# Head products that take both halves of x in one pass, in halves of 256 columns

## What is computed

```python
z = rms_norm(x, norm_mix) @ w_in      # first block, 2048 -> 5144 columns
# columns: gMLP 1024, dilated attention 3 x 512, NSA queries 1024,
#          keys and values for compression 512, selection 512, window 512, gates 24
# later: cross attention (q from x, k and v from mem), MLP of 8192
p_lat = h_lat @ w_in_2                # second block: HGRN2 queries 1024, gates, values, ...
```

## Time and profile before

| | |
|---|---|
| median of 3 executions | 2600.96 us (2600.3 to 2600.99) |
| the profiled execution | 2600.4 us, span 2598.6 us |
| TensorE busy | 2576.3 us, 99% |
| VectorE, ScalarE busy | 1838.8 us (71%), 1361.8 us (52%) |
| moved by DMA | 582.98 MB, mean 224 GB/s |

### The profile page before, as it was taken

The page is one execution under the profiler, slowest core; times in us unless marked ns, Lnnn a source line. Parts: engine busy times, 40 slices in busy tenths (PEclk is TensorE's granted clock), DMA queues, the critical chain, the costliest instruction groups (busy, mean ns, idle before and its releaser), DMA issues.

```text
span 2598.6 us, 35433 instructions
## 1 busy us (share of the span) xinstructions
PE 2576.3 (99%) x13200; PEld 2173.1 (84%) x13200; DVE 1838.8 (71%) x3327; ACT 1361.8 (52%) x2613; POOL 176.9 (7%) x233
## 2 busy tenths in 40 slices
PE   8999999999999999999999999999999999999999
PEld 7999889888888888888888898888788888888887
DVE  5677665777799999676867775677866665555555
ACT  5445575655545445455766566565544444444443
POOL 1011100021100000000011100000001111000000
PEclk9999999999999999999999999999999999999999
DMA  9796665688888888866777755544577777565564
GB/s 304 236 296 184 209 202 171 188 287 278 290 284 270 277 285 271 308 191 219 237 242 236 247 175 153 156 131 153 162 233 257 255 253 224 186 195 188 188 193 161
DMA packets 315707, 582.98 MB, mean 224 GB/s; under 512 B 30176, under 2 KB 38384, under 8 KB 315408
## 3 DMA queue, kind: packets, MB, share of 16 engines
q1 hardware_dynamic: 296768, 559.94, 66.0%
q0 software_dynamic: 18480, 20.47, 3.6%
q10 hardware_dynamic: 288, 0.31, 0.0%
HBM read 574.35 MB, written 2.10 MB: 222 GB/s over the span
## 4 chain that ended last, share of the span: by engine, by line
PE 96%; DVE 1%; ACT 1%; SPq 0%; DMA 0%; issue 0%; DVEq 0%; ACTq 0%
PE ps L1838 27%; PE ps L1840 26%; PE ps L1839 26%; PE ps L1827 3%; PE ps L1828 3%; PE ps L1829 3%; PE ps L1784 2%; PE ps L1920 1%; PE ps L1890 1%; PE ps L1909 1%; DMA raw<-in_w_in 0%; DVE wlo L2495 0%; PE ps L2035 0%; ACT whi L2157 0%; PE ps L2052 0%
## 5 line engine op out<-in xcount | busy, mean ns | idle before, releaser
L2495 DVE TENSOR_TENSOR wlo<-raw,whi 128x512 fp32r<-128x512 f32 x1712 | 1098.2, 686 | 536.5 <-ACT whi L2157 534.0
L2157 ACT ACTIVATE whi<-raw 128x512 fp32r<-128x512 f32 x1712 | 982.0, 624 | 817.1 <-PE ps L1840 527.1
L1838 PE MATMUL ps<-whi,th 128*128 128x512 f32 (+1 forms) x3124 | 1230.9, 394 | 2.2 <-ACT hA L2351 1.0
L1840 PE MATMUL ps<-whi,tl 128*128 128x512 f32 (+1 forms) x3124 | 1211.2, 388 | 0.0
L1839 PE MATMUL ps<-wlo,th 128*128 128x512 f32 (+1 forms) x3124 | 1210.3, 387 | 0.0
L1838 PEld LDWEIGHTS ps<-whi,th 128*128 128x128 f32 x3124 | 586.9, 188 | 122.2 <-issue 5.1
L1840 PEld LDWEIGHTS ps<-whi,tl 128*128 128x128 f32 x3124 | 586.5, 188 | 121.7
L1839 PEld LDWEIGHTS ps<-wlo,th 128*128 128x128 f32 x3124 | 587.4, 188 | 115.7 <-issue 1.0
L2513 DVE SCALAR_TENSOR_TENSOR acc<-raw,silc,acc 128x512 f32<-128x512 f32 x480 | 343.9, 746 | 10.5 <-DMA raw<-in_w_mod 6.0
L1827 PE MATMUL ps<-th,whi 128*128 128x256 f32 x640 | 186.0, 291 | 11.0 <-DVE wlo L2495 8.1
L1828 PE MATMUL ps<-th,wlo 128*128 128x256 f32 x640 | 181.6, 284 | 0.0
(11 more groups left out here) (320 smaller groups left out, 1296.7 us busy)
## 6 DMA issues: line engine op xcount, KB each, us to landing
raw<-in_w_in SPq DMA_DIRECT2D x231, 512.0 KB, 3.9
raw<-in_w_down SPq DMA_DIRECT2D x216, 512.0 KB, 4.6
raw<-in_w_mod SPq DMA_DIRECT2D x192, 512.0 KB, 4.5
raw<-in_w_gate_up SPq DMA_DIRECT2D x176, 512.0 KB, 3.5
raw<-in_w_up SPq DMA_DIRECT2D x128, 512.0 KB, 4.6
raw<-in_w_out SPq DMA_DIRECT2D x64, 512.0 KB, 3.8
raw<-in_xattn_wkv SPq DMA_DIRECT2D x16, 512.0 KB, 3.4
raw<-in_w_in SPq DMA_DIRECT2D x16, 268.0 KB, 4.1
```

Source lines behind the costliest of these rows:

```text
L1838: pe.matmul(p, xh, wh[:, c, c0:n], start=a and (form != "both" or tb == 0), stop=False, skip_group_check=True)
L1840: ins = pe.matmul(p, xl, wh[:, c, c0:n], start=False, stop=z, skip_group_check=True)
L2157: self.e.activation(t.his[g % NHI][:, n * c:n * c + n], t.raws[j % NRAW][:, n * c:n * c + n], ACT.Copy).then_inc(*s.hi.up((g, c)))
L2495: self.e.tensor_tensor(t.los[j % NRAW][:, at], t.raws[j % NRAW][:, at], t.his[g % NHI][:, at].bitcast(F), ALU.subtract).then_inc(*s.lo.up( ...
```

## The change

In form "heads" a gemm now walks its 512 columns in two halves of 256: each half runs over all 16 k-tiles with a pair of banks of its own, one head in each bank. `th` and `tl` lie in one tile (`thl`), so that one product with the standing `whi` moves 512 columns, th and tl of a k-tile: hi by hi lands in the first half of the bank, hi by lo (of x) in the second. A second product, of 256 columns, with `wlo` standing, adds to the first half. At the end of each half ScalarE copies the second half of each bank into the destination, VectorE adds the first, and then VectorE multiplies by the scales (or ScalarE applies silu). Chunks of 256 columns hold four k-tiles (the first two chunks: two), in rows of 1 KB. For cc the multiply by the scales is moved into `first_steps`, behind the spreading of the scales. "rows", "both" and "three" stay.

```diff
@@ gemm
+        if form == "heads":
+            for b in range(n // 256):
+                pair = self.take_pair()
+                epi(b, pair, self.part(op, w, row0, col0 + 256 * b, 256, kts, pair, form))
+            return
@@ part
-            m = 1 if self.small else min({512: 2, 536: 1}.get(n, len(kts)), len(kts) - i)
+            m = {512: 2, 536: 1, 256: 4}[n]
+            m = min(m // 2 if self.small else m, len(kts) - i)
@@ direct
-        def epi(pair, end):
-            for b in range(nh // 2):
-                self.heads_direct(name, b, pair, end, dst[:, h0 + 2 * b:h0 + 2 * b + 2, :], by, used)
-            pair.give((self.s.hx, (name, nh // 2 - 1)))
-            self.flags.add(name)
+        def epi(b, pair, end):
+            out = dst[:, h0 + 2 * b:h0 + 2 * b + 2, :]
+            self.heads_joined(name, b, pair, end, out, used)
+            pair.give((self.s.hj, (name, b)))
+            if late:
+                self.flags.add(f"{name} joined {b}")
+                return
+            self.heads_scaled(name, b, out, by)
+            if 2 * b + 2 == nh:
+                self.flags.add(name)
@@ first_steps
-            self.spread("x", op1.rs)
+            while not self.side_ready():
+                yield
+            bank = self.side().take()
+            self.spread_rstd("x", op1.rs, bank)
+            bank.give((s.sd, "x"))
+            yield from self.until("cc joined 1")
+            for b in range(2):
+                self.heads_scaled("cc", b, t.cc[:, 2 * b:2 * b + 2, :], op1)
+            self.flags.add("cc")
@@ Tensor.multiply
+        if form == "heads":
+            for c, kt in enumerate(kts):
+                self.wait_ge(*s.lo.at((g, c // 2)))
+                self.wait_all(op.ready[kt])
+                a, z = first and c == 0, last and c == len(kts) - 1
+                for h in range(2):
+                    hs = slice(128 * h, 128 * h + 128)
+                    pe.matmul(pair.tile[h][:, :], wh[:, c, hs], op.hl[:, :, kt, :], start=a, stop=False, skip_group_check=True)
+                    ins = pe.matmul(pair.tile[h][:, 0:S], wl[:, c, hs], op.h[:, kt, :], start=False, stop=z, skip_group_check=True)
+            ins.then_inc(*s.mm.up(j))
+            return
@@ Scalar
+    def heads_joined(self, name, b, pair, end, dst, used):
+        self.wait_all([end])
+        self.wait_all(used)
+        for h in range(2):
+            ins = self.e.activation(dst[:, h, :], pair.tile[h][:, S:2 * S], ACT.Copy)
+        ins.then_inc(*self.s.hb.up((name, b)))
+    def heads_silu(self, name, b, dst):
+        self.wait_ge(*self.s.hj.at((name, b)))
+        self.e.activation(dst, dst, ACT.Silu).then_inc(*self.s.hqs.up((name, b)))
@@ Vector
+    def heads_joined(self, name, b, pair, end, dst, used):
+        t, s = self.t, self.s
+        self.wait_ge(*s.hb.at((name, b)))
+        for h in range(2):
+            ins = self.e.tensor_tensor(dst[:, h, :], pair.tile[h][:, 0:S], dst[:, h, :], ALU.add)
+        ins.then_inc(*s.hj.up((name, b)))
```

More of the change, by code:

```diff
@@ L112, in __init__ @@
             new("turn_hi"), new("turn_lo"))
-        self.hqs = new("queries_silu")
+        self.hqs, self.hb, self.hj = new("queries_silu"), new("heads_second_half"), new("heads_joined")
         self.ro, self.hx = new("rows_copied"), new("heads_direct")
@@ L163, in __init__ @@
         self.name = name
-        self.h, self.l = tiles
+        self.h, self.l, self.hl = tiles
         self.ready = [[] for _ in range(16)]
@@ L239, in __init__ @@
         for n, at in (("1", r_1), ("2", r_2), ("3", z)):
[L240 removed]
+            both = sb("thl" + n, at, [2, 16, S], R)
+            self.op[n] = (both[:, 0, :, :], both[:, 1, :, :], both)
         self.yr = sb("yr", r_1 + 16384, [16, S])
@@ L770, in rows, with direct, epi @@
         return epi
-    def direct(self, name, dst, h0, by, nh=4, used=()):
-        def epi(pair, end):
-            for b in range(nh // 2):
-                self.heads_direct(name, b, pair, end, dst[:, h0 + 2 * b:h0 + 2 * b + 2, :], by, used)
-            pair.give((self.s.hx, (name, nh // 2 - 1)))
-            self.flags.add(name)
+    def direct(self, name, dst, h0, by, nh=4, used=(), late=False):
+        def epi(b, pair, end):
[8 more added lines that the diff above has]
+                self.flags.add(name)
         return epi
     def silu_heads(self, name, dst, used):
[L783 to L786, removed]
+        def epi(b, pair, end):
+            self.heads_joined(name, b, pair, end, dst[:, 2 * b:2 * b + 2, :], used)
+            self.heads_silu(name, b, dst[:, 2 * b:2 * b + 2, :])
+            pair.give((self.s.hj, (name, b)))
+            if b:
+                self.flags.add(name)
         return epi
@@ L1328, in run @@
         w_in = a["w_in"][0]
-        self.gemm(op1, w_in, 0, 3584, 512, range(16), self.direct("cc", t.cc, 0, op1), "heads")
+        self.gemm(op1, w_in, 0, 3584, 512, range(16), self.direct("cc", t.cc, 0, op1, late=True), "heads")
         self.spawn("big", self.compress())
@@ L1805, in multiply @@
         wh, wl = view(t.his[g % NHI], (len(kts), n)) if self.plan else None, view(t.los[j % NRAW], (len(kts), n)) if self.plan else None
-        heads = {"rows": 0, "heads": n // 128, "both": n // 256, "three": 2}[form]
+        heads = {"rows": 0, "heads": 2, "both": n // 256, "three": 2}[form]
         c0 = 128 * heads
@@ L2155, in split @@
             self.wait_ge(*signal.at(key))
-        for c in range(k):
-            self.e.activation(t.his[g % NHI][:, n * c:n * c + n], t.raws[j % NRAW][:, n * c:n * c + n], ACT.Copy).then_inc(*s.hi.up((g, c)))
+        u = 2 if n == 256 else 1
+        for c in range(0, k, u):
+            at = slice(n * c, n * (c + u))
+            self.e.activation(t.his[g % NHI][:, at], t.raws[j % NRAW][:, at], ACT.Copy).then_inc(*s.hi.up((g, c // u)))
     def stat(self, name, tb, src, landed, at):
@@ L2491, in split @@
         k, n = self.plan[j][2]
-        for c in range(k):
-            at = slice(n * c, n * c + n)
-            self.wait_ge(*s.hi.at((g, c)))
+        u = 2 if n == 256 else 1
+        for c in range(0, k, u):
+            at = slice(n * c, n * (c + u))
+            self.wait_ge(*s.hi.at((g, c // u)))
             self.e.tensor_tensor(t.los[j % NRAW][:, at], t.raws[j % NRAW][:, at], t.his[g % NHI][:, at].bitcast(F),
-                                 ALU.subtract).then_inc(*s.lo.up((g, c)))
+                                 ALU.subtract).then_inc(*s.lo.up((g, c // u)))
     def mod_add(self, jj, j, kc, vs):
```

11 lines of the change are left out of this document (6 added, 5 removed).

## The result

The changed kernel takes 2607.47 us (median of 9 runs, 2604.77 to 2608.98), the kernel before 2600.96 beside it (9 runs, 2600.2 to 2603.01). The ratio is 1.0025, with a 95% interval of 1.0016 to 1.0033: slower by 6.5 us, where no change was forecast, and 2.5 us above the upper end of the forecast range (2594.5 to 2605.0). The profiled execution took 2607.2 us (span 2605.4).

What follows compares the result with a forecast made beforehand. TensorE's products and waits were taken to bound the kernel. From 2600.4 us, +6.5 first gemm, -1.8 given back, +1.6 half rate, -6.8 other gemms make -0.5: 2599.9, stated as 2600.0 us; range 2594.5 to 2605.0.

Steps and rivals of the forecast that it cites:

- first gemm, with half rate: Start: last x part late, first product of rows 6.5 us later; 3.15 us at half rate after the idle, 1.6 us.
- wait for cb given back: At 46.63 us: TensorE's wait for blocks VectorE makes from cc goes, 1.8 us less (0 if VectorE is late).
- pairs of the eight other gemms: Gemms after the first: a pair takes 0.347 us where three products took 0.360; 512 x 0.0133 = 6.8 us less.
- query halves: Ends of the query gemms' halves: copies, additions and silu nearly hidden; 0 to 2 us a half, costed at nothing.
- 41.5 to 44: Sign for the forecast at the start: first product of rows comes at 41.5 to 44 us.
- rival A: First gemm: no late start, the whole product gain stays, 2592.7 us; chance 0.10.
- signs that were to show the prediction wrong: Pair step not 0.347, k-tiles 14 and 15 starting before 28, or new waits over 1 us behind query halves.
- rival B: Four query halves: ScalarE's queue of copies, table loads and silu outlasts the cover; 2 us each give 2608; chance 0.07.
- The cover named: Ends of halves: three chunks already converted, 8.3 us of products, hide the copies and additions.

Runs made afterwards that it cites:

- experiment 8: Changed kernel with every pair made as three products of 256 columns into the same banks, halves kept: 2610.01 us (5 runs).
- experiment 9: Changed kernel with the last part of x (k-tiles 14 and 15) made ahead of the squares and of the conversion of weight chunk 7: 2601.12 us, ratio 1.0001.
- experiment 4: Changed kernel with the compression starting one chunk of rows earlier, as it did before the change: 2604.61 us, ratio 1.0015.
- experiment 1: Changed kernel with the last part of x (k-tiles 14 and 15) made ahead of the sums of squares only: 2606.66 us, ratio 1.0022.
- experiment 10: Kernel of experiment 9 with the query gemms hq0 and hq1 in their old form: 2600.76 us.
- experiment 11: Kernel of experiment 9 with weight chunk 7 loaded ahead of the four loads of x by rows: 2601.51 us.
- experiment 3: Changed kernel with the query gemms hq0 and hq1 in their old form: 2606.5 us; its trace is of an execution of 2608.71 us.
- 5: Changed kernel with 22 extra products of 512 columns, result overwritten, in TensorE's pause ahead of k-tile 14 of the first gemm: 2603.18 us.
- 12: Kernel of experiment 10 with the compression one chunk of rows earlier: 2602.04 us.
- experiment 6: Changed kernel with cc, hq0 and hq1 in their old form and the other six gemms in the new one: 2597.78 us, ratio 0.9986.
- 2: Changed kernel with only the first gemm (cc) in its old form: 2598.11 us, ratio 0.9989.

## Why the prediction was wrong

By its own terms, measured on the profiled executions (the medians differ by 6.5):

| term of the sum | forecast | measured | by |
|---|---|---|---|
| first gemm, with half rate | +6.5 + 1.6 = +8.1 | +8.76 | 1st product of rows |
| wait for cb given back | -1.8 | -2.24, of which the wait 1.84 | 17th against 1st |
| what lies behind, near 110 us | no term | +3.72 | 85th against 17th |
| pairs of the eight other gemms | 512 x 0.0133 = -6.8 | 512 x 0.010 = -5.2 | experiment 8 |
| query halves | 0 | +1.8 | wait at 1402, second half of `hq0` |
| sum | -0.5 | +6.8 | last product: +6.78 |

**The first gemm was right**, mechanism and size: idle 6.1 us up to 30.0 (forecast 6 to 7 up to 30), the steps of .43 and .21 behind it, no wait for cb. Only the half rate lasted 4.3 us in place of 3.15, which makes 2.15 us for 1.6, and the first product of rows came at 44.97, 1 us past the 41.5 to 44 that was to show it. What the prediction read wrongly there is how firm it was. It said in rival A that "the change brings nothing forward", and the part in question had landed at 19.3; experiment 9 has it made 8 us sooner (20.9 instead of 29.0) with two edits of order.

**The step that failed is "Given back"**, and the sum that ends with it. The prediction saw that four chunks of rows instead of three would stand ahead of the compression, and booked only the wait that this removes, with no term for what lies behind: 3.7 us came there. The compression doesn't only multiply: it takes its chunks of `cmp_v` from the same queue of loads as the weights and `w_mod`, and its later place changes the order in that queue. In the changed kernel the chunk of `w_in` that VectorE needs next was issued at 99.9 and landed at 103.7, behind `cmp_v` at 96.8; with the compression in its old place it was issued at 96.8 and landed at 102.4. Near 110 us, where the turned operand stands on VectorE behind work on these chunks, that decides whether 0.45 or 1.85 us of pause come. That the place matters is shown by experiment 4 (2.9 us less by the medians, 0.67 in place of 3.72 us in this stretch); the way over the load queue is read from two traces. Nor was the later place needed for what was booked: in experiment 4 the wait for cb stayed away without it. Of the 3.7 us the longer pause is 1.9; the rest is 3.8 us at a granted clock of 0.55, and that part is not bound to the order. Experiment 1, the same program from there on and as late a start, had a pause of 1.67 us, no fall of the clock, and 2.1 us where the changed kernel had 3.7.

**The pair was over-valued by a quarter.** The step of 0.347 was right where it holds, but a pair's step has two values: in `cq1` the changed kernel's execution has 0.347 throughout, that of experiment 1 0.353 throughout, and three products have 0.360 there (experiment 8). Over the eight gemms, steps of over 0.5 us left out, the mean is 0.352 for the pair and 0.363 for the three; by gemm it is 0.347 to 0.357 and 0.360 to 0.368. Why the step changes from stretch to stretch is open. The prediction took its gain from the better value and multiplied it by 512; the error of 0.003 makes 1.6 us. The Trainium skill's value for the fixed part ("TensorE: Matmul & The Clock Gate", Back-to-back issue gap; about 2.5 ns) would have given an estimate of 1.3 us for these 512 where the runs have 5.2.

**Query halves at nothing** was the lower end of 0 to 2 us a half. One half of four paid 1.8, and a wait of over 1 us there was among the signs that were to show the prediction wrong. It came by another way than rival B's: the copies (0.66 us) and additions (0.76) were in B's sum, but what made TensorE wait for them was not a queue with table loads in it, it was the ring of two pairs, of which one was still in use. The cover named, three chunks already converted, doesn't help when the wait is for a bank.

None of the rivals came true. B had the sign and, by accident, the time: 2608, from 2 us for each of four query halves, where one half paid. From the first product of rows to the end the prediction had 2554 us and the run took 2560.4, so most of its error lies behind the first gemm. Its last line has a slip of its own, too small to matter: 2599.9 and the 0.6 of the median make 2600.5, not 2600.0.

**What stays open.** Whether the clock falls after a pause differs between executions with little else between them. Near 110 us: not after pauses of 1.32 and 1.67 us, nor after 2.39 in experiment 10, but after 1.85, 1.96 (experiment 11) and 2.76 (experiment 3). At 18.5 us eleven kernels with the new first gemm have the same pause of 1.9 to 2.1 us, and half rate follows within 1.5 us in four executions (experiments 3, 4, 5 and 12) and not in the other seven. In the kernel before, 2.23 us ahead of 29.5 had no fall behind them; in experiment 6, 2.13 us ahead of 30.0 had (granted clock 0.60 from 30.0 to 34.3). A fall costs 1.7 us or more in these traces, as much as several of the effects above. Nor was it tried to give the query halves a third pair of banks.

## To carry to other kernels

When a step moves to another place in the program, follow what it loads, not only what it computes: look 60 us further on at what stands ahead of it in the load queue and behind which wait on VectorE and ScalarE it lands. Before taking an engine's wait for bound by loads, look for work in its queue whose data are already there, and move that ahead of all the waits in front of it: one removed alone shows nothing. And a saving of 10 ns a pair is made only where TensorE never waits: it paid here in the six gemms in the middle and in `hq1` (0.7 us), and was outweighed by waits in `cc` and `hq0`.

## What the runs showed that I had not expected

- The pause of 6.06 us cost its own length and 2.15 us of clock behind it, 4.3 us at 0.50; filling it with products whose result nobody reads brought the kernel 4.3 us, by 2.4 at once and the rest 70 us later.
- The changed kernel's 9 runs span 4.2 us, the 11 of experiment 4 1.5. A second fall of the clock in some runs and not in others would do that, and the two quickest of the 9 have a granted clock of 0.999 where the rest have 0.997 or 0.998. But only one run of each has a trace, and experiments 9 and 10, with no fall in theirs, span 4.2 and 4.3 us, so it isn't shown.
- The eighth chunk of weights landed at very different times behind the same loads on its own queue, and what differs is another queue. GpSimd issues eleven loads of constants, the first of them `lmk`, once VectorE has made the sixth part of x. In eight executions it issued `lmk` at 20.7 to 21.5, and the chunk landed at 26.5 to 27.3; in experiments 6, 2, 10 and 9 at 20.3, 20.0, 19.4 and 19.5, and it landed at 27.0, 28.0, 29.1 and 29.2. In experiment 12 it was 20.1 and 30.0, with the loads ahead of it some 0.6 us later as well. So the mended start, which makes the parts of x sooner, seems to let in sooner what then delays the chunk. No run held these loads back, and the cause is not shown. Timelines of GpSimd in the changed kernel and in experiment 9:

```profile
21.10 0.54 POOL L1725 DMA_DIRECT2D lmk<-in_consts  x1 [17.50 <-DVE thl L2537]
...
19.48 0.54 POOL L1727 DMA_DIRECT2D lmk<-in_consts  x1 [15.89 <-DVE thl L2539]
```
